# Moving TensorE's activations off the 512-byte grid of the weights, in a two-layer decoder trunk

## The reference

```python
for i in range(DEPTH):                      # DEPTH = 2
    h = _rmsnorm(x, attn_norm_g[i])
    if i % N_MIXERS == 0:                   # layer 0: 16 heads of 128, no softmax
        mix = _stick_breaking_attention(h, sb_w_qkv[j], sb_w_o[j])
    else:                                   # layer 1: indexer, top-64 keys, 4 kv heads
        mix = _dsa_attention(h, dsa_w_in[j], ..., dsa_w_o[j])
    x = x + mix
    h = _rmsnorm(x, ffn_norm_g[i])
    x = x + _conv_ffn(h, ffn_w_up[i], ffn_conv_w[i], ffn_conv_b[i], ffn_w_down[i])
```

## Time and profile before

| | |
|---|---|
| median of 3 runs | 2236.75 us (2236.71 to 2236.8) |
| the profiled execution's own time | 2236.73 us |
| its span in the profile | 2234.9 us |
| TensorE busy | 2225.6 us, 13130 matmuls |
| VectorE busy | 1496.8 us |
| ScalarE busy | 1166.7 us |
| granted TensorE clock | 1.000 |

### The profile page before, as it was taken

How to read it: one execution, slowest core, us unless ns; L and a number is a source line. 1 busy time by engine, 2 the same in 40 slices (tenths; PEclk the granted TensorE clock), 3 DMA queues, 4 the chain that set the end, 5 groups by cost and what they waited for, 6 DMA issues and landing times. The chain is left out here.

```text
span 2234.9 us, 36154 instructions
## 1 busy us (share of the span) xinstructions
PE 2225.6 (100%) x13130; PEld 1972.3 (88%) x13130; DVE 1496.8 (67%) x1778; ACT 1166.7 (52%) x1400; POOL 2.5 (0%) x9
## 2 busy tenths in 40 slices
PE   9999999999999999999999999999999999999999
PEld 8999998888888888888889888888888888888888
DVE  7655556677777777555578887667777777774444
ACT  7555555555555555444455456555555555553332
POOL 0000000000000000000000000000000000000000
PEclk9999999999999999999999999999999999999999
DMA  7545455555555556555666544455555555556654
GB/s 259 169 161 175 161 169 186 189 185 187 192 192 184 189 186 197 189 190 190 191 205 199 179 151 131 151 179 184 193 192 185 187 192 193 187 189 205 199 193 137
DMA packets 113537, 411.97 MB, mean 184 GB/s; under 512 B 12736, under 2 KB 13376, under 8 KB 113472
## 3 DMA queue, kind: packets, MB, share of 16 engines
q1 hardware_dynamic: 112464, 407.49, 55.5%
q10 hardware_dynamic: 576, 1.97, 0.2%
q0 software_dynamic: 432, 1.57, 0.2%
HBM read 408.88 MB, written 2.10 MB: 184 GB/s over the span
## 5 line engine op out<-in xcount | busy, mean ns | idle before, releaser
L584 DVE TENSOR_TENSOR w_lo<-raw,w_hi 128x1024 fp32r<-128x1024 f32 x772 | 937.6, 1223 | 681.7 <-ACT w_hi L261 676.0
L1026 PE MATMUL psum<-xg,w_hi 128*128 128x512 f32 (+1 forms) x3936 | 1359.8, 391 | 1.7 <-DVE xg L599 1.7
L261 ACT CAST w_hi<-raw 128x1024 fp32r<-128x1024 f32 x772 | 803.9, 1049 | 784.0 <-PE psum L1026 780.2
L1026 PE MATMUL psum<-xg,w_lo 128*128 128x256 f32 (+1 forms) x3936 | 1094.4, 278 | 0.0
L1026 PEld LDWEIGHTS psum<-xg,w_hi 128*128 128x128 f32 x3936 | 736.6, 187 | 156.4 <-issue 2.2
L1026 PEld LDWEIGHTS psum<-xg,w_lo 128*128 128x128 f32 x3936 | 744.3, 189 | 2.4 <-issue 2.2
L1026 PE MATMUL psum<-hid,w_hi 128*128 128x512 f32 x1408 | 488.2, 391 | 0.0
L1026 PE MATMUL psum<-hid,w_lo 128*128 128x256 f32 x1408 | 394.2, 280 | 0.0
L1026 PEld LDWEIGHTS psum<-hid,w_hi 128*128 128x128 f32 x1408 | 263.3, 187 | 57.7
L1026 PEld LDWEIGHTS psum<-hid,w_lo 128*128 128x128 f32 x1408 | 266.1, 189 | 0.0
L1026 PE MATMUL psum<-att,w_hi 128*128 128x512 f32 x512 | 180.0, 396 | 0.1
(11 more groups left out here) (152 smaller groups left out, 912.8 us busy)
## 6 DMA issues: line engine op xcount, KB each, us to landing
raw<-w_all SPq DMA_DIRECT2D x772, 512.0 KB, 3.4
xres<-x_in SPq DMA_DIRECT2D x4, 512.0 KB, 7.1
cst<-consts_in ACTq DMA_DIRECT2D x2, 768.0 KB, 5.9
out_t<-xres POOLq DMA_DIRECT2D x3, 512.0 KB, 4.0
out_t<-xres SPq DMA_DIRECT2D x4, 128.0 KB, 1.8
vecs<-vecs_in ACTq DMA_DIRECT2D x1, 354.0 KB, 6.5
avg_d<-consts_in SPq DMA_DIRECT2D x1, 64.0 KB, 9.2
vecs<-vecs_in ACTq DMA_DIRECT2D x1, 32.0 KB, 4.1
```

The lines of the kernel that those rows point to most:

```text
L261: act.copy(w_hi[:, c % RING, :], raw[:, c % RING, :]).then_inc(hi_ready, 1)
L584: dve.tensor_tensor(w_lo[:, c % RING, :], raw[:, c % RING, :], f32(w_hi[:, c % RING, :]), ALU.subtract).then_inc(lo_ready, 1)
L1026: return pe.matmul(o, lhsT, rhs, start=start, stop=True, skip_group_check=True)
```

## The change

Three tensors that nothing writes or reads are put into the SBUF row: 64 float32 (256 bytes) ahead of xg, 32 (128 bytes) ahead of hid, and 8 (32 bytes) ahead of att. xg moves by 256 bytes, and so does all that follows it up to gates; hid moves by 256 + 128 = 384 bytes; att by 256 + 32 = 288, and so do the attention's own tensors behind it. raw, w_hi, w_lo and xres stay. No instruction changes but for these addresses.

```diff
         xres = sb("xres", [P, KT, T])
+        xg_gap = sb("xg_gap", [P, 64])
         xg = sb("xg", [P, KT, 2 * T], F32R)
...
         with ExitStack() as mlp:
+            hid_gap = sb("hid_gap", [P, 32], F32, mlp)
             hid = sb("hid", [P, FT, 2 * T], F32R, mlp)
         att_ctx = ctx.enter_context(ExitStack())
+        att_gap = sb("att_gap", [P, 8], F32, att_ctx)
         att = sb("att", [P, NH, 2 * T], F32R, att_ctx)
```

## The result

The changed kernel takes 2244.12 us (median of 7 runs, 2243.82 to 2244.42) against 2236.75 us. The ratio is 1.0035, 95% interval 1.0026 to 1.0044. I had forecast 2236.7 us and no change, with a chance of 0.18 on slower. The time lies within my range, on the side that I thought least likely.

What follows compares the result with a forecast made beforehand. TensorE's matmul pairs were taken to bound the kernel; 0 for instructions, addresses, ScalarE, VectorE and DMA added to 2236.7 us leaves 2236.7 us. The range was 2213 to 2256 us, with 0.60 on staying within 0.2%.

Steps and rivals of the forecast that it cites:

- TensorE's pairs alone set the time: Whole kernel: 5600 wide-plus-narrow matmul pairs on TensorE, mostly about 346.7 ns each, fill the span; other engines and DMA cost 0.
- The address term: TensorE's matmul pairs: moving xg, hid and att off the 512-byte grid was taken to cost 0 us.
- the slow rhythm: Second pair rate in the old trace: 353.3 ns, 6.67 ns above the fast one, on 634 of 5600 pairs, none in MLP loops.
- the readings: Four arguments from the old trace that a matmul pair's price doesn't hang on operand addresses.
- The first: Rows differ in every address bit from 512 bytes up, yet all 1408 wide hid matmuls last 391 ns, so no bank effect.
- The second: Slow and fast rates occur with the same operands at the same addresses, so what ran before decides, not where data lie.
- The third: With xg stationary and weights moving, matmuls take 226.7 ns: the same 13.3 ns overhead per weight load, whatever is stationary.
- The fourth: Index projection already starts moving rows 256 bytes in; its 285 ns pairs show neither gain nor loss beyond 5 ns.
- the 45 ns: Index projection pair's overhead beyond 240 ns of columns, explained by a short matmul not covering the next weight load.
- The faster one: The offset removes a collision of weight load and moving read: 23.5 us less (wide hid) to 51 us (hid, att); chance 0.22.
- The slower rival: MLP loops fall into the 353.3 ns rate: hid 9.4 us more, xg 18.8, both 28.2; chance 0.18.
- The attention stages: Only these stages' 1376 pairs change rate: 4.2 us less to 4.9 us more; chance 0.05.

## Why the prediction was wrong

*That TensorE's pairs alone set the time* held: the whole difference lies in them, and neither ScalarE, VectorE nor DMA moved the end. (The 780.2 us of ScalarE that I called its longest wait are the sum of 564 waits, the longest of 2.3 us; it is ahead all the same.)

*The address term.* I took 0 for all three tensors; "no row shows an offset of 32 or 128 bytes in these operands ... again I take 0" is the step that failed, for hid. It measured 2 x 3.1 = 6.2 us. For xg at 256 the 0 was right, and the index projection, which has that distance, was the right row, though with its shorter rows it could only bound the effect. For att at 288 it was right within the noise (2235.02 us against 2236.33 beside it); what att's place does is to keep the output projections out of the slow rhythm.

*Why the readings misled.* The first (rows alike over slots, blocks and tiles) excludes only steps of 512 bytes and more; the pattern repeats every 256 bytes as far as tried, so every row of the old trace stood at distance 0 or 256 and none could show it. I had written this limit down and priced the rest at nothing by argument. The second, that both rhythms occur at one address and hence none matters, was a wrong conclusion from a right observation. What ran before picks among the rhythms that a distance allows, and the distance decides which ones those are: two at 0 (346.7 and 353.3 ns), at 16 and 32 only the fast one was seen in the long stages, at 384 one of 351.1. The third, the same 13.3 ns with the roles exchanged, stood at distance 0 as well: with xg at 32 or 384 bytes the 96 matmuls of layer 1's value projection come 233 ns apart and not 227. The fourth held for 256 bytes, the one distance that it had, but its account of the 45 ns was right in the sum by luck: I had put 176.7 ns on the wide index matmul and 103 to 112 on the narrow one, and in that same timeline the narrow one starts about 0.20 us behind the wide one and the next wide one 0.09 behind it.

*The rivals.* The faster one fell: eight distances within 256 bytes, none under 346.7 ns a pair, where the gain had been priced down to 320. The Trainium skill, "TensorE: Matmul & The Clock Gate", "Step-by-step: what each phase is for", says that loading the next weights "doesn't steal SBUF read bandwidth from the running matmul". Here the price of the same two instructions goes from 346.7 to 353.3 ns with the distance of their operands alone, and doesn't change when both are moved together; the measurement decides. That the two reads collide is the reading that fits, but no run shows the collision itself.
The slower rival had the right place and sign for hid, 9.4 us by the slow rhythm's 6.67 ns; at 384 bytes it is another rhythm, of 4.4 ns and 6.2 us. I gave this rival 0.18 because none of 4224 pairs was slow, which told of the places before and not of the new ones. That the time lies within my range is owed to the width of the range: its centre assumed that addresses have no effect.

*The attention stages.* I saw their rhythm as free to change by some us either way. The changed kernel loses 2.2 and 0.7 us in the Q, K and V stages, where xg's move has no part (308.35 and 145.01 us alone) and the tensors behind att do (310.12 and 145.69 with att, 311.43 and 145.77 without). I had named the products of those tensors only as a row to read, not as something that moves. Layer 1's output projection won back 1.4, which the kernel at the old distances can also win by itself.

*Left open:* which of the attention's tensors keeps the slow stretches alive, and what within TensorE makes the prices 346.7, 350.0, 351.1 and 353.3 ns.

## What to carry to other kernels

Where weight loads run beneath matmuls and TensorE is the bound, the distance between the moving rows and the weight blocks can be a parameter of the time. In this kernel (fp32r, rows of 512 and 256 columns) it is worth 1.9% of a pair, and 1.0% of the time in the worst kernel tried; other types weren't tried, and with other shapes or roles the cheap distances differ (32 bytes). Choose it on purpose, and look again after any change to what is allocated ahead. A row that is constant over all addresses tried says nothing about distances that no address tried has: ask which residues the rows cover before pricing the others at nothing. And two steady rates of one instruction pair in a trace are a warning that a stage's price may depend on what ran before it.

## What the runs showed of the hardware that I had not expected

- The price of a pair (512 and 256 columns in fp32r, each with a weight load) depends on the distance of the operands, with a period of 256 bytes as far as tried: 346.7 ns at 0, 16 and 32, 353.3 at 48, 64 and 192, 350.0 at 96, 351.1 at 128. It does so in the last microseconds too, where no other engine and no DMA is busy (351 against 347 ns).
- With the roles exchanged, a matmul of 512 columns takes 227 ns at distance 0 and 233 at 32 and at 384.
- At distance 0 there are two rates that keep themselves up. hid's 1408 pairs ran at 346.7 ns in the kernel before and at 353.3 behind up projections with xg at 384 bytes, with the same operands at the same distance.
- The kernel before has two times 1.6 us apart from run to run (2235.1 and 2236.7), just what layer 1's output projection and the stage behind it differ by between the two rates; with att alone at 288 bytes, or xg and att at 32, all runs lie within 1 us.
